# Attention with 64-row heads: scores of a tile's two heads formed separately, in a new order on TensorE

## The reference

```
def block_attention(q, k, v):          # per block of 128 queries
    s = einsum('bqkgd,btkd->bkgqt', q_blk, k) * ATTN_SCALE
    p = softmax(s, axis=-1)
    return einsum('bkgqt,btkd->bqkgd', p, v)
```

## Time and profile before

| | |
|---|---|
| median of 3 runs | 2402.37 us (2398.77 to 2404.18) |
| the profiled execution | 2404.98 us, span 2403.0 us |
| TensorE busy over the span | 2165.9 us (90%) |
| VectorE busy | 1130.6 us (47%) |
| ScalarE busy | 827.4 us (34%) |
| GpSimd busy | 317.5 us (13%) |
| mean granted TensorE clock | 0.959 |

### The profile page before, as it was taken

How to read it: one execution, slowest core, us unless ns; L and a number is a source line. 1 busy time by engine, 2 the same in 40 slices (tenths; PEclk the granted TensorE clock), 3 DMA queues, 4 the chain that set the end, 5 groups by cost and what they waited for, 6 DMA issues and landing times. The chain is left out here.

```text
span 2403.0 us, 58388 instructions
## 1 busy us (share of the span) xinstructions
PE 2165.9 (90%) x26083; PEld 1856.5 (77%) x26083; DVE 1130.6 (47%) x2062; ACT 827.4 (34%) x1480; POOL 317.5 (13%) x542
## 2 busy tenths in 40 slices
PE   6999768888999999979995888888896989999999
PEld 3678544468999999944884776777775789999998
DVE  3142566445432342163515777777773354324421
ACT  4242444333211121171324555565553232112211
POOL 1000230010000001100002444343441100000000
PEclk8999999989999999979997999999997989999999
DMA  7221209921222222021110000000001222222221
GB/s 267 71 71 38 73 5 322 329 89 53 71 75 84 71 71 81 26 69 63 70 36 11 7 9 6 7 10 9 9 6 37 73 70 71 75 84 71 71 80 53
DMA packets 160741, 167.72 MB, mean 70 GB/s; under 512 B 13788, under 2 KB 117996, under 8 KB 160364
## 3 DMA queue, kind: packets, MB, share of 16 engines
q1 hardware_dynamic: 160492, 164.00, 21.2%
HBM read 160.44 MB, written 3.54 MB: 68 GB/s over the span
## 5 line engine op out<-in xcount | busy, mean ns | idle before, releaser
L168 PE MATMUL psum<-arena 64*64 64x64 f32 (+6 forms) x17072 | 835.4, 247 | 139.0 <-DVE arena L1969 16.0
L168 PEld LDWEIGHTS psum<-arena 64*64 64x64 f32 (+3 forms) x17072 | 665.8, 145 | 350.9 <-issue 159.5
L648 ACT ACTIVATE weights_high<-weights 128x2048 fp32r<-128x2048 f32 x62 | 118.6, 1913 | 335.3 <-PE psum L168 335.3
L168 PE MATMUL psum<-hidden_high,weights_high 128*128 128x320 f32 x1024 | 233.4, 309 | 0.0
L168 PE MATMUL psum<-hidden_low,weights_high 128*128 128x320 f32 x1024 | 233.3, 309 | 0.0
L168 PE MATMUL psum<-hidden_high,weights_low 128*128 128x320 f32 x1024 | 233.3, 309 | 0.0
L168 PE MATMUL psum<-norm_high,weights_high 128*128 128x320 f32 x992 | 226.9, 310 | 0.0
L168 PE MATMUL psum<-norm_low,weights_high 128*128 128x320 f32 x992 | 226.8, 310 | 0.0
L168 PE MATMUL psum<-norm_high,weights_low 128*128 128x320 f32 x992 | 226.7, 310 | 0.0
L711 DVE SCALAR_TENSOR_TENSOR arena<-psum,ada,arena 128x320 f32<-128x320 f32 (+2 forms) x96 | 36.3, 434 | 314.9 <-PE psum L168 314.9
L168 PEld LDWEIGHTS psum<-hidden_low,weights_high 128*128 128x128 f32 x1024 | 171.2, 188 | 0.0
(11 more groups left out here) (213 smaller groups left out, 2838.4 us busy)
## 6 DMA issues: line engine op xcount, KB each, us to landing
weights<-in_mlp_w SPq DMA_DIRECT2D x64, 1024.0 KB, 5.8
arena<-in_ada_w SPq DMA_DIRECT2D x24, 2048.0 KB, 9.3
arena<-in_ab_w_in SPq DMA_DIRECT2D x6, 2048.0 KB, 7.8
arena<-in_ab_w_out SPq DMA_DIRECT2D x2, 2048.0 KB, 10.6
arena<-in_rwkv_wv SPq DMA_DIRECT2D x2, 2048.0 KB, 8.5
arena<-in_rwkv_wr SPq DMA_DIRECT2D x2, 2048.0 KB, 8.0
arena<-in_rwkv_wk SPq DMA_DIRECT2D x2, 2048.0 KB, 7.9
arena<-in_rwkv_wo SPq DMA_DIRECT2D x2, 2048.0 KB, 10.6
```

Source lines behind the costliest of these rows:

```text
L168: return nc.tensor.matmul(out, lhsT, rhs, start=start, stop=stop, skip_group_check=shared)
L648: A.activation(WHI[:, g % 2, :], WRAW[:, g % 2, :], ACT.Copy).then_inc(S("mlp_weights_high"), 1)
```

## The change

The scores of a step are formed by two calls, one for each head. Each waits only for the exponential of its own head of the step before, and each raises `att_scores`, so that the row maximum of a head waits for that head alone. On TensorE the values of step m-1 stand between the two. The set of matmuls is the same.

```diff
         def attn_pe(pe):
-            def scores(m):
+            def scores(m, h):
                 hp, t = ATT[m]
+                r = HALF[h]
                 if m:
-                    pe.wait_ge(S("att_exp"), 2 * m)
+                    pe.wait_ge(S("att_exp"), 2 * (m - 1) + h + 1)
                 for c0, n, b in ((0, NS, 0), (NS, NP_, 1)) if t < 4 else ((T, NP_, 0),):
-                    for h, r in enumerate(HALF):
-                        ins = mm(PS[:, 2 * h + b, 0:n], unit(U_Q + hp)[r, 128 * t:128 * t + 128], KD[r, hp // 2, c0:c0 + n])
+                    ins = mm(PS[:, 2 * h + b, 0:n], unit(U_Q + hp)[r, 128 * t:128 * t + 128], KD[r, hp // 2, c0:c0 + n])
                 ins.then_inc(S("att_scores"), 1)
...
-            scores(0)
+            scores(0, 0)
+            scores(0, 1)
             for m in range(NA):
                 if m + 1 < NA:
-                    scores(m + 1)
+                    scores(m + 1, 0)
                 if m:
                     values(m - 1)
+                if m + 1 < NA:
+                    scores(m + 1, 1)
                 turn(m)
...
             def row_max(m):
                 k = keys_of(ATT[m][1])
-                dve.wait_ge(S("att_scores"), m + 1)
                 for h in range(2):
+                    dve.wait_ge(S("att_scores"), 2 * m + h + 1)
                     st = att_small(m, h)
```

## The result

The changed kernel takes 2422.33 us (median of 5, 2416.92 to 2429.51), the kernel before in the same comparison 2404.0 (median of 5, 2398.77 to 2408.01): a ratio of 1.008, with an interval of 1.0067 to 1.0093. Measured a second time it had 2418.56 against 2405.36, ratio 1.0059 (1.0037 to 1.0081). It is slower, as forecast, but by 18.3 us in place of 10.1 (by 13.2 the second time), and the first median lies above the range, which ended at 2419.

What follows compares the result with a forecast made beforehand. The loop of GpSimd, TensorE's transposes and VectorE's copies was taken to set the full tile's 5.00 us pace. Terms 3.8 + 5.2 + 1.05 = 10.1 us, against 2402.37, gave 2412.5 us; range 2404.5 to 2419.

Steps and rivals of the forecast that it cites:

- GpSimd, transposes and copies bound a full tile, and the scores have 2 us of slack: Full tiles: the loop GpSimd, TensorE, VectorE sets the 5.00 us pace; exponentials finish 2.0 us before the reciprocals needing them.
- A lone head takes as long as the pair: Score matmuls on TensorE: each head formed alone takes about 1.35 us, so forming them apart costs 1.35 more per full tile.
- Eight full-tile steps, 0.48 each: Full tiles: transposes queue behind head 1's scores, start at R+2.66 instead of R+2.18; 8 x 0.48 = 3.8 us.
- Steps before a context tile, nothing: m = 3, 8, 13, 18: head 1's 256-column scores end near R+1.8, inside GpSimd's time; cost nothing.
- Context tiles, 1.75 each: m = 4, 9, 14: head 1's late maximum delays copies and the next reciprocal; 3 x 1.75 = 5.2 us.
- The step behind, nothing: Step after a context tile (m = 5, 10, 15): next reciprocal at R+5.38, before 5.38; nothing gained.
- The start, +1.05: Stage start, at half clock: tile 1's head 1 maximum and the transposes come late; next reciprocals +1.05 us.
- The sum, 10.1 us: Whole attention stage: 3.8 + 5.2 + 1.05 = 10.1 us, all passed on to the execution time.
- Rival 1: Stage start: the clock stays at 2.4 GHz, a gain of 1.9 instead of a loss of 1.05; 2409.6 us, chance 0.32.
- Rival 2: Score matmuls: a lone head takes half the pair's time and the clock stays up; not slower, about 2402, chance 0.07.
- Rival 3: Score matmuls: a lone head's four weight loads of 0.19 stand free, making it 2.0 us; about 2424, chance 0.08.
- rival 4: Later stages, shifted by 10 us, meet their clock falls differently: a few us of either sign; no chance of its own.

Runs made afterwards that it cites:

- e4: Kernel before with head 1's transposes issued ahead of head 0's, which wait for GpSimd: 2398.77 against 2403.09 us, ratio 0.9977.
- e2: Changed kernel with the values moved behind both heads' scores, heads still formed apart but next to each other: 2399.74 against 2403.09 us, ratio 0.9988.
- e3: Kernel before with the values of m-1 moved ahead of the pair of scores of m+1, heads together: 2435.94 against 2403.09 us, ratio 1.013.
- g4: Kernel before with one more GpSimd instruction of 128 columns ahead of each scaling of a full tile: 2413.35 against 2404.39 us, ratio 1.0035.
- e1: Changed kernel with each head's scores contracted over all 128 partitions, not 64 (timing only): 2407.03 against 2403.09 us, ratio 1.0018.

## Why the prediction was right or wrong

- *GpSimd, transposes and copies bound a full tile, and the scores have 2 us of slack:* right. e4 left the scores' work as it was, shortened the loop and gained; the finer waits of e2 gained nothing in a full tile.
- *A lone head takes as long as the pair:* right where the head is alone. Head 1 between values and transposes takes 1.28 us of TensorE's stream. It was taken too widely at the start: heads that are issued apart, but with nothing between, run side by side.
- *Eight full-tile steps, 0.48 each:* right, 0.47. *Steps before a context tile, nothing:* right, 5.01. *Context tiles, 1.75 each:* right, 1.73, and 1.74 when undone. *The step behind, nothing:* right, 5.37.
- *The start, +1.05:* wrong, nothing (the first step is 7.18 in both kernels). The half-clock stretch there began as before but lasted 17.1 us instead of 6.9, which lengthened the second step to 9.51.
- *The sum, 10.1 us:* the step that failed is the silent one that all its durations rest on: that TensorE would run at full clock through the stage because it did in the rows of before. The clock inside the stage was a term put at nothing, without a reason; I let it change only at the start and behind the stage (rivals 1 and 4). It cost 11.2 us inside the stage in the profiled execution, as much as the whole forecast. The cause is shown as far as the filled kernel goes: with work on the idle half of the array beside head 1's scores, twice, the falls behind the start were gone and the stage was 99.9 and 100.2 us instead of 110.7 and 112.3. That the clock can also fall with full pairs, at steps of 6.1 us, is shown by e3. That the kernel before stood near a fall, and that g4's one fall belongs to its longer steps, is my reading and is not shown.
- *Rival 1 (the clock doesn't fall at the start):* the opposite happened. Its premise, 2.5 us of work with tile 0's heads one after the other, did not come about, as the two ran side by side in 1.36. With heads over all partitions (e1) they did run one after the other; there the clock stayed up and the first step was 5.01.
- *Rival 2 (a lone head takes half):* no; the transposes start at R+2.66.
- *Rival 3 (weight loads stand free):* no; they run under the matmuls of the same head. The Trainium skill ("TensorE: Matmul & The Clock Gate", Part 3, The mechanism) says loads overlap running matmuls only in another row group; this trace does not agree (loads of 0.19 us start at 302.76 and 303.19, just behind the starts of two of head 1's own matmuls, and the next matmuls follow those starts by 0.43 and 0.11). The same section says that TensorE pulls a load ahead of running matmuls when it is for a non-conflicting row group or for the background weight buffer; e2's 1.36 us for eight matmuls agrees with the first, and there the matmuls of the two halves overlap as well. Which of the two holds for the lone head's loads no run here shows.
- *The later stages:* 5.0 us less than before in this execution, more than the 2 us that the prediction named as a sign of being wrong. Between the profiles of this study the time from GpSimd's last start in the stage to the end varied from 2043.9 to 2053.8 us. It is 2043.9 to 2046.3 in the six kernels and repeats in which the values stand between the heads' scores, and 2046.1 to 2053.8 in the other six. It goes in part with the clock, which stood at half behind that start for 165.1 us in the changed kernel and 177.0 before: the few us of rival 4. Over the twelve profiles the two numbers have a correlation of 0.76; why the falls there differ stays open. In the profiled executions the stage grew by 20.2 us and the time by 15.0 (2419.99 against 2404.98) for this reason, and the filled kernel's stage grew by 9.4 and its time by 2.8.

## What to carry to other kernels

Before counting durations at full clock, ask whether the change makes TensorE's steps longer or leaves part of the array empty. In these runs either came with falls of the clock (e3, and the changed kernel against the filled one), so the clock belongs in the sum as a term of its own; here it was 11.2 us against 10.1 for all others. A useful test is to fill the idle half of the array with work that is thrown away, and to read the granted clock: here the kernel became faster and the half-clock stretches behind the start went. And before splitting a producer to start its consumer earlier, look at which loop sets the pace: here the split work had 2 us of slack, while a swap of the two heads' transposes in the loop that binds gave 0.2% (e4).

## What the runs showed of the hardware that was not expected

- Added matmuls shortened the run. With 68 more instructions on the idle half of the array, 2408.09 against 2418.56 us beside it on the same chip.
- Four matmuls of one head followed by four of the other, on different partitions, took 1.36 us together, as when they alternate, with a semaphore step between the two heads (e2, and tile 0 of the changed kernel).
- At half clock a full-tile step took 9.52 us and not 5.48. TensorE's whole stream is then the path: 7.26 us for both heads' scores and the values, and the transposes behind them, from 268.07 to the next group at 277.59. The scores of head 0, which cost nothing at full clock, cost all of their time there.
